# Six raw weight buffers in place of seven, four rounded ones in place of three, and both splits made three units ahead instead of two

## The chip, the cores and the metric

The kernel runs on one core of one Trainium2 chip. The metric is the device time of one execution in microseconds (us). Kernels are compared by runs that alternate on the same chip.

## What is computed

Two layers (`DEPTH = 2`) over 256 context tokens and 256 latent tokens of width 1024. Every matrix product with a large weight is an fp32 product. Cut to what matters:

```
for l in range(DEPTH):
    mod_l, mod_c = split(silu(c) @ w_ada[l] + b_ada[l], 6), split(silu(c_ctx) @ w_ada[l] + b_ada[l], 6)
    h_l, h_c = modulate(rms_norm(x, g), ...), modulate(rms_norm(ctx, g), ...)
    p_l, p_c = split_proj(h_l @ w_in[l]), split_proj(h_c @ w_in[l])
    gla, att, lru = gla_branch(...), attention_branch(...), rglru_branch(...)
    y = sum(sigmoid(gate_i) * (branch_i @ w_branch[l, i]) for i in range(3)) @ w_out[l]
    x = x + mod_l[2] * rms_norm(y, g_post_mix)                 # ctx too, in layer 0
    h = modulate(rms_norm(x, g_pre_ffn), ...)
    u = depthwise_conv(h @ ffn_w_up[l]); g, v = split(u, 2)
    x = x + mod_l[5] * rms_norm((silu(g) * v) @ ffn_w_down[l], g_post_ffn)
```

`w_ada` (1024 x 6144 for each layer) gives the modulation. It is a product with two vectors only, but its weights are 50 MB for the two layers.

## The kernel before

**Units and pairs.** All large weights but `w_ada` are cut into units of 512 KB (`UK = 4` tiles of 128 rows by `UC = 256` columns). Two units (six for `down`) make a pair: 256 output columns, summed over all of the input rows, in two banks of PSUM. There are 352 units. Their order is `PAIR_ORDER`, once for each layer: the projections of the branches, then `y`, `g2` and `b2` in turn, `out`, `up` (22 pairs) and `down`. I write `up 2.0` for the first unit of pair `up 2`, and `up 2.1` for its second. Pairs use two places in PSUM in turn (`PAIR[q % 2]`), so a pair can start on TensorE (PE) only when the pair two before it has been taken out of PSUM (`taken`).

**The split.** A product is made of three passes: a weight is split into a rounded part (`whi`, made by ScalarE, ACT, in `hi(u)`, L397) and the rest (`wlo`, made by VectorE, DVE, in `lo(u)`, L743). The raw weight comes by DMA into one of `RAW` buffers, `wlo` is written over it, and `whi` goes to one of `HI` buffers. So a raw buffer is in use from the issue of its DMA until PE has used the unit (`w_unit_used`, `s_used`).

**The ring.** All DMAs of weights are issued by SyncE (SP) in the order of the list `RING`, in which entry n uses raw buffer `n % RAW`. SP waits before each until the entry that had the buffer before is done with:

```
for n, (kind, v, r) in enumerate(RING):
    s = n % RAW
    if n >= RAW:
        prev, pv, pr = RING[n - RAW]
        if prev == "w":
            sp_.wait_ge(s_used, pv + 1)
        else:
            sp_.wait_ge(s_round, 2 * pv + pr // 2 + 1)
```

**The modulation weights in the ring.** While layer 0 runs from `y 0` to `down 0`, 20 chunks of `w_ada` pass through the same buffers, one for every four units. Let B be the unit at which a chunk is based (`ADA_RUN`: `y 0.0`, `y 2.0`, `g2 0.0` to `g2 3.0`, `out 0.0`, `out 2.0`, `up 0.0`, `up 2.0` to `up 20.0`, `down 0.0`). A chunk has four entries a0 to a3 of 512 KB. PE uses a0 and a1 in a round behind unit B (`ada_round`, L1195) and a2 and a3 in a second round behind unit B+1, and it sends the result through a small product (`ada_pick`, L1204) behind unit B+3. In the ring a0 and a1 stand behind the weights of B+2, and a2 and a3 behind those of B+3. PE runs its instructions in order: a round that waits for its DMA holds everything behind it.

**Edges.** ACT and DVE run their parts of the stream at an `edge(u)` for each unit. ACT's is this (DVE's is alike, with `lo` for `hi`, and with `copy_rows` and `take_mod` of the modulation chunk placed by `u + LEAD - 4` and `u + LEAD - 6`):

```
if q >= 0:
    evac_first(q)
if u + LEAD < NU:
    hi(u + LEAD)
if q >= 0:
    evac_second(q)
```

`q` is the pair that ended with unit u-1, if one did. So a pair is taken out of PSUM at the edge of the unit behind it, and the rounded part of unit u + `LEAD` is made at the edge of u. ACT and DVE run in order too. `hi(u)` waits for the raw buffer's DMA, and for `s_used >= u - HI + 1`.

Of the kernel before, what the change touches and what calls it, by code (L numbers as in the profile page):

```python
# [34 lines left out]
D_FF = 2816  # L35
FT = D_FF // P
UK, UC = 4, 256
RAW, HI, LEAD = 7, 3, 2


PCOLS = {}
# [1622 lines left out]
```

## Time and profile before

| | |
|---|---|
| Three runs | 2107.59 us median (2105.42 to 2109.31) |
| The profiled execution | 2108.57 us, its span 2106.7 us |
| PE busy | 1975.7 us, 94% |
| PE weight load busy | 1605.9 us, 76% |
| DVE busy | 1130.2 us, 54% |
| ACT busy | 940.5 us, 45% |
| DMA, mean | 116 GB/s; 352 raw weight DMAs and 80 of `w_ada`, 512 KB each |
| Chain that ended last | PE 81%, DVE 10%, ACT 5%, issue 2%, DMA 1% |

Busy is the time in which an engine runs instructions; matmuls are pipelined and their ends are modelled. The span is that of the slowest core's instructions, and the execution's time is 1.9 us more.

### The profile page before, as it was taken

How to read it: one execution, taken by the hardware profiler on the slowest of the kernel's cores; microseconds unless marked ns; L12 is line 12 of the kernel's file. 1: busy time of each engine (PE TensorE's matmuls, PEld its weight loads, DVE VectorE, ACT ScalarE, POOL GpSimd, SP SyncE). 2: the span in 40 equal slices, each digit the busy share in tenths (PEclk: the TensorE clock that was granted, in tenths of full speed). 3: DMA queues.
4: the chain of work that ended last, by engine and by line, in shares of the span. 5: the costliest groups of instructions: out<-in, count | busy, mean ns of one | idle time of the engine just before them, and what ended most of it. 6: DMA issues, size and time to landing. Idle time of an engine off the chain costs nothing.

```text
span 2106.7 us, 26324 instructions
## 1 busy us (share of the span) xinstructions
PE 1975.7 (94%) x10944; PEld 1605.9 (76%) x10944; DVE 1130.2 (54%) x1617; ACT 940.5 (45%) x1301; POOL 18.3 (1%) x49
## 2 busy tenths in 40 slices
PE   4999999999999999799999998799898999989997
PEld 1878766777777777477777786588676888979997
DVE  2566455544645333455555323666545678657864
ACT  2343344454654322333333223444343787546653
POOL 1000000000000000000000000000000000000000
PEclk8999999999999999999999999899999999999999
DMA  7211111123332544235444433121221444545663
GB/s 285 61 61 51 56 50 41 49 92 95 96 97 85 177 170 163 104 105 177 169 175 175 167 101 94 41 71 60 76 60 51 155 156 154 177 125 161 181 187 103
DMA packets 67510, 244.97 MB, mean 116 GB/s; under 512 B 7600, under 2 KB 8640, under 8 KB 67264
## 3 DMA queue, kind: packets, MB, share of 16 engines
q1 hardware_dynamic: 64544, 233.86, 34.1%
q0 software_dynamic: 1696, 5.24, 0.8%
q10 hardware_dynamic: 1152, 4.19, 0.5%
q8 instruction: 87, 1.43, 0.3%
q14 instruction: 31, 0.25, 0.0%
HBM read 242.21 MB, written 1.05 MB: 115 GB/s over the span
## 4 chain that ended last, share of the span: by engine, by line
PE 81%; DVE 10%; ACT 5%; issue 2%; DMA 1%; SPq 0%; ACTq 0%; DVEq 0%
PE ps L1264 61%; PE ps L1254 4%; PE ps L1195 2%; PE ps L1540 2%; PE ps L1450 2%; DVE wlo L743 1%; PE ps L1284 1%; DMA wraw<-in_weights 1%; DVE state L1004 1%; PE ps L1471 1%; PE ps L1204 1%; PE ps L1364 1%; ACT whi L397 1%; PE ps L1374 1%; PE ps L1351 1%
## 5 line engine op out<-in xcount | busy, mean ns | idle before, releaser
L743 DVE TENSOR_TENSOR wlo<-wraw,whi 128x1024 fp32r<-128x1024 f32 x352 | 429.6, 1223 | 497.2 <-ACT whi L397 496.7
L397 ACT ACTIVATE whi<-wraw 128x1024 fp32r<-128x1024 f32 x352 | 370.9, 1055 | 396.4 <-PE ps L1264 252.0
L1264 PE MATMUL ps<-hh,whi 128*128 128x512 f32 (+1 forms) x1760 | 416.5, 359 | 25.2 <-DVE hl L860 23.2
L1264 PE MATMUL ps<-hl,whi 128*128 128x512 f32 (+1 forms) x1760 | 399.0, 349 | 0.0
L1264 PEld LDWEIGHTS ps<-hh,whi 128*128 128x128 f32 x1760 | 293.3, 194 | 101.8 <-issue 64.2
L1264 PE MATMUL ps<-hh,wlo 128*128 128x512 f32 (+1 forms) x1760 | 365.5, 349 | 1.8 <-DVE wlo L743 1.8
L1264 PEld LDWEIGHTS ps<-hl,whi 128*128 128x128 f32 x1760 | 295.9, 192 | 42.5 <-issue 2.2
L1264 PEld LDWEIGHTS ps<-hh,wlo 128*128 128x128 f32 x1760 | 286.1, 191 | 44.5 <-issue 4.4
L771 DVE SCALAR_TENSOR_TENSOR fa<-ps,par,fa 128x510 f32<-128x510 f32 (+1 forms) x176 | 100.0, 610 | 14.5 <-ACT fa L460 12.9
L1264 PE MATMUL ps<-bh,whi 128*128 128x512 f32 (+1 forms) x384 | 85.2, 344 | 0.4 <-ACT whi L397 0.4
L460 ACT ACTIVATE fa<-ps,par 128x512 f32<-128x512 f32 (+1 forms) x88 | 54.0, 664 | 69.1 <-PE ps L1264 69.0
L1264 PE MATMUL ps<-bl,whi 128*128 128x512 f32 (+1 forms) x384 | 82.2, 336 | 0.0
L1264 PE MATMUL ps<-fh,whi 128*128 128x512 f32 (+1 forms) x352 | 78.9, 342 | 0.0
L1264 PE MATMUL ps<-fl,whi 128*128 128x512 f32 (+1 forms) x352 | 76.7, 336 | 0.0
L1264 PE MATMUL ps<-bh,wlo 128*128 128x512 f32 (+1 forms) x384 | 74.4, 336 | 0.0
L1264 PEld LDWEIGHTS ps<-bh,whi 128*128 128x128 f32 x384 | 62.4, 190 | 13.8 <-issue 6.2
L749 DVE COPY ada_rows<-ps 128x512 f32<-128x512 f32 x24 | 16.6, 690 | 104.3 <-PE ps L1195 104.3
L1264 PE MATMUL ps<-fh,wlo 128*128 128x512 f32 (+1 forms) x352 | 68.8, 336 | 0.0
L1264 PEld LDWEIGHTS ps<-bl,whi 128*128 128x128 f32 x384 | 62.5, 190 | 7.6
L1264 PEld LDWEIGHTS ps<-bh,wlo 128*128 128x128 f32 x384 | 60.8, 190 | 7.5
L1264 PEld LDWEIGHTS ps<-fh,whi 128*128 128x128 f32 x352 | 57.5, 190 | 9.7 <-issue 3.1
L1264 PEld LDWEIGHTS ps<-fl,whi 128*128 128x128 f32 x352 | 57.6, 190 | 6.9
(206 smaller groups left out, 2392.8 us busy)
## 6 DMA issues: line engine op xcount, KB each, us to landing
wraw<-in_weights SPq DMA_DIRECT2D x352, 512.0 KB, 3.6
wada<-in_w_ada SPq DMA_DIRECT2D x80, 512.0 KB, 4.3
ada_first<-in_w_ada ACTq DMA_DIRECT2D x8, 512.0 KB, 18.5
ada_first<-in_w_ada SPq DMA_DIRECT2D x8, 512.0 KB, 19.9
wgate<-in_w_gate POOLq DMA_DIRECT2D x16, 256.0 KB, 2.8
x<-in_xt SPq DMA_DIRECT2D x1, 2048.0 KB, 9.9
out_x<-x SPq DMA_DIRECT2D x1, 1024.0 KB, 4.5
par<-in_params POOLq DMA_DIRECT2D x1, 370.0 KB, 9.4
```

The costliest lines, as they stand in the source:

```text
L397: A_(whi[u % HI][:], wraw[RING_W[u] % RAW][:], ACT.Copy).then_inc(s_hi, 1)
L460: ins = A_(fa[j][:, f, c0:], pair_[:, f, c0:], ACT.Identity, scale=pcol(l, "fw")[:, t + 2 * FT:t + 2 * FT + 1], bias=pcol(l, "fb")[:, t:t ...
L743: V.tensor_tensor(wlo[s][:], wraw[s][:], whi[u % HI][:].bitcast(F32), ALU.subtract).then_inc(s_lo, 1)
L771: return V.scalar_tensor_tensor(o[:, :, a], v[:, :, b], pcol(l, name)[:, tile:tile + 1], o[:, :, a], ALU.mult, ALU.add)
L1004: ins = V.scalar_tensor_tensor(state[:, d, p + 1], state[:, d, p], g_end[:, d, c:c + 1], kv_, ALU.mult, ALU.add)
L1195: ins = mm(ps[32 * j:32 * j + 32, k if k < 4 else 5, :], csil32[:, 4 * r + j, :], w[:, j % 2, :], start=r == 0, stop=r == 1, tile_position ...
L1204: ins = mm(ps[:, 4, 2 * f:2 * f + 2], ada_rows[:, f * P:(f + 1) * P], pick[:], start=True, stop=True)
L1254: ins = mm(dst[:, r // 2, 256 * (r % 2):256 * (r % 2 + 1)], x_[:, UK * h + kk, r * P:(r + 1) * P], w[:, kk, :], start=first, stop=h == m - ...
L1264: ins = mm(dst[:, r, c:], w[:, kk, r * P:(r + 1) * P], x_[:, UK * h + kk, c:], start=h == 0 and k in (0, 2) and kk == 0, stop=h == m - 1 a ...
L1284: ins = mm(ps[:, 6, c0:], ones[:], src[:, k, c0:], start=k == 0, stop=k == KT - 1)
L1450: ins = mm(ps[:, 4 + t, 0:(g + 1) * CTX], aq[:, h, r0:r0 + P], ak[:, h // (AQ // AKV), 0:(g + 1) * CTX], start=True, stop=True)
L1540: ins = mm(ps[:, 4 + 2 * d + g], wgate[:, 2 * d + g, :], xc[:, n, :], start=True, stop=True)
```

## The change

One line:

```diff
-RAW, HI, LEAD = 7, 3, 2
+RAW, HI, LEAD = 6, 4, 3
```

A buffer has 4 KB in each partition on both sides, so all that lies behind the buffers in SBUF stays where it was. `hi(u + LEAD)` waits at edge u for `s_used >= u` before and after the change. No instruction is added or removed. What is waited for moves, and so does the place of both splits in their engines' rows.

The waits of the ring follow from the code above. For the entries around a base B (before: the entry seven back, now: six back):

| entry | waits for, 7 buffers | waits for, 6 buffers |
|---|---|---|
| w(B+2) | a0 of the chunk before | a1 of the chunk before |
| a0 | a1 of the chunk before | w(B-1) |
| a1 | w(B-1) | a2 of the chunk before |
| w(B+3) | a2 of the chunk before | a3 of the chunk before |
| a2 | a3 of the chunk before | w(B) |
| a3 | w(B) | w(B+1) |
| w(B+4) | w(B+1) | w(B+2) |
| w(B+5) | w(B+2) | a0 |
| w(B+6) | a0 | a1 |

Each row of SP below is one DMA. `wraw` is a unit's weight and `wada` an entry of a chunk. `w_unit_used` is a wait for a unit, `ada_rounds_done` one for a round. The place is base B = `up 2.0`. The rows are w(B+2), a0, a1, w(B+3), a2, a3, w(B+4), w(B+5), w(B+6). Before:

```order
L325 DMA wraw3_57<-in_weights 128x1024 [waits ada_rounds_done]
L327 DMA wada4_72<-in_w_ada 128x1024 [waits ada_rounds_done]
L327 DMA wada5_73<-in_w_ada 128x1024 [waits w_unit_used]
L325 DMA wraw6_60<-in_weights 128x1024 [waits ada_rounds_done]
L327 DMA wada0_68<-in_w_ada 128x1024 [waits ada_rounds_done]
L327 DMA wada1_69<-in_w_ada 128x1024 [waits w_unit_used]
L325 DMA wraw2_56<-in_weights 128x1024 [waits w_unit_used]
L325 DMA wraw3_57<-in_weights 128x1024 [waits w_unit_used]
L325 DMA wraw4_58<-in_weights 128x1024 [waits ada_rounds_done]
```

The same nine DMAs of SP now:

```order
L325 DMA wraw0_54<-in_weights 128x1024 [waits ada_rounds_done]
L327 DMA wada1_67<-in_w_ada 128x1024 [waits w_unit_used]
L327 DMA wada2_68<-in_w_ada 128x1024 [waits ada_rounds_done]
L325 DMA wraw3_57<-in_weights 128x1024 [waits ada_rounds_done]
L327 DMA wada4_70<-in_w_ada 128x1024 [waits w_unit_used]
L327 DMA wada5_71<-in_w_ada 128x1024 [waits w_unit_used]
L325 DMA wraw0_54<-in_weights 128x1024 [waits w_unit_used]
L325 DMA wraw1_55<-in_weights 128x1024 [waits ada_rounds_done]
L325 DMA wraw2_56<-in_weights 128x1024 [waits ada_rounds_done]
```

The order stands; a2 now waits for a unit, and w(B+5) for a round.

On ACT at the same place, before: `hi` of B+3, the first part of the evacuation of `up 2` (`fa0`, at the edge of B+2), `hi` of B+4, the rest of the evacuation, `hi` of B+5, and the evacuation of `up 3`.

```order
L397 ACTIVATE whi1_76<-wraw6_60 128x1024 [waits w_unit_used,raw_full6]
L460 ACTIVATE fa0_129<-ps,par 128x512 [waits split_pairs_made,w_unit_used]
L460 ACTIVATE fa0_129<-ps,par 128x512
L397 ACTIVATE whi2_77<-wraw2_56 128x1024 [waits w_unit_used,raw_full2]
L480 ACTIVATE fs0_131<-fa0_129 128x512 [waits pair0_taken]
L482 ACTIVATE fh_127<-fa0_129 128x512 [waits product_made]
L397 ACTIVATE whi0_75<-wraw3_57 128x1024 [waits w_unit_used,raw_full3]
L460 ACTIVATE fa1_130<-ps,par 128x512 [waits split_pairs_made,w_unit_used]
```

And now:

```order
L397 ACTIVATE whi0_72<-wraw0_54 128x1024 [waits w_unit_used,raw_full0]
L460 ACTIVATE fa0_127<-ps,par 128x512 [waits split_pairs_made,w_unit_used]
L460 ACTIVATE fa0_127<-ps,par 128x512
L397 ACTIVATE whi1_73<-wraw1_55 128x1024 [waits w_unit_used,raw_full1]
L480 ACTIVATE fs0_129<-fa0_127 128x512 [waits pair0_taken]
L482 ACTIVATE fh_125<-fa0_127 128x512 [waits product_made]
L397 ACTIVATE whi2_74<-wraw2_56 128x1024 [waits w_unit_used,raw_full2]
L460 ACTIVATE fa1_128<-ps,par 128x512 [waits split_pairs_made,w_unit_used]
```

The `hi` ahead of the evacuation of `up 2` was that of B+3 and is now that of B+4, whose weight is the DMA into `wraw0` above.

On DVE at the start of layer 0, ahead of the first use of the modulation, before:

```order
L911 TENSOR_TENSOR lrl<-lrw,lrh 128x8x2x16
L743 TENSOR_TENSOR wlo_61<-wraw_54,whi_75 128x1024
L743 TENSOR_TENSOR wlo_62<-wraw_55,whi_76 128x1024
L749 COPY ada_rows<-ps 128x512
L755 TENSOR_TENSOR mod<-ps,par 128x8
```

And now:

```order
L911 TENSOR_TENSOR lrl<-lrw,lrh 128x8x2x16
L743 TENSOR_TENSOR wlo_60<-wraw_54,whi_72 128x1024
L743 TENSOR_TENSOR wlo_61<-wraw_55,whi_73 128x1024
L743 TENSOR_TENSOR wlo_62<-wraw_56,whi_74 128x1024
L749 COPY ada_rows<-ps 128x512
```

A third split stands ahead of `copy_rows(0)` (L749).

## Rows read from the trace of the kernel before

**Rows 1.** The page: TensorE busy, and its granted clock in 40 slices.
```profile
PE 1975.7 (94%) x10944; PEld 1605.9 (76%) x10944; DVE 1130.2 (54%) x1617; ACT 940.5 (45%) x1301; POOL 18.3 (1%) x49
PEclk8999999999999999999999999899999999999999
```

**Rows 2.** Waits of PE, whole span: us in total, times, longest.
```profile
PE ps L1264 <- DVE hl L860: 23.2, 3, 9.7
...
PE ps L1264 <- DVE wlo L743: 1.8, 1, 1.8
...
PE ps L1264 <- ACT whi L397: 0.9, 2, 0.5
```

**Rows 3.** Waits of ACT, stretch 645 to 1205 us.
```profile
ACT whi L397 <- DMA wraw<-in_weights: 139.5, 43, 8.7
```

**Rows 4.** Timeline around base `up 2.0`: start, length, what [idle before, releaser].
```profile
939.19 1.07 PE L1195 MATMUL ps<-wada,csil 128*32 128x512 f32 x8
939.29 7.47 SPq L325 DMA_DIRECT2D wraw<-in_weights  x3
...
940.19 1.20 PE L1264 MATMUL ps<-hh,whi 128*128 128x512 f32 x4
...
942.95 1.06 ACT L397 ACTIVATE whi<-wraw 128x1024 fp32r<-128x1024 f32 x1 [2.20 <-DMA wraw<-in_weights]
...
945.77 1.07 PE L1264 MATMUL ps<-hh,whi 128*128 128x512 f32 x4
...
949.57 1.06 ACT L397 ACTIVATE whi<-wraw 128x1024 fp32r<-128x1024 f32 x1 [3.03 <-DMA wraw<-in_weights]
...
951.41 1.45 ACT L460 ACTIVATE fa<-ps,par 128x512 f32<-128x512 f32 x2 [0.78 <-PE ps L1264]
...
952.01 1.19 PE L1264 MATMUL ps<-hh,whi 128*128 128x512 f32 x4
...
952.89 2.85 DVE L771 SCALAR_TENSOR_TENSOR fa<-ps,par,fa 128x510 f32<-128x510 f32 x4 [1.00 <-ACT fa L460]
```

**Rows 5.** The tile `wada`: time from the issue of a DMA to its landing.
```profile
DMA to landing us min/median/max: 3.3/4.3/7.0
```

**Rows 6.** DMA issues at 738.24 to 739.09 us, three together: the last.
```profile
wada<-in_w_ada SPq DMA_DIRECT2D x1, 512.0 KB, 5.9
```

**Rows 7.** Timeline in `out 3`, base `out 2.0`: PE's sum of squares, and ACT.
```profile
863.73 1.88 PE L1284 MATMUL ps<-sqm,ones 128*128 128x512 f32 x4
...
865.57 1.06 ACT L397 ACTIVATE whi<-wraw 128x1024 fp32r<-128x1024 f32 x1 [5.55 <-DMA wraw<-in_weights]
```

**Rows 8.** Timeline behind `b2 3` (813.74 on), and behind `out 3` (869.28 on).
```profile
813.74 0.33 SPq L327 DMA_DIRECT2D wada<-in_w_ada  x1
...
821.03 1.20 PE L1264 MATMUL ps<-mh,whi 128*128 128x512 f32 x4
...
869.28 1.02 ACT L449 ACTIVATE sqm<-ps 128x1024 f32<-128x1024 f32 x1 [2.65 <-PE ps L1264]
...
871.10 1.06 ACT L397 ACTIVATE whi<-wraw 128x1024 fp32r<-128x1024 f32 x1
```

**Rows 9.** Timeline of the start.
```profile
33.23 2.48 DVE L743 TENSOR_TENSOR wlo<-wraw,whi 128x1024 fp32r<-128x1024 f32 x2 [5.39 <-ACT whi L397]
...
36.35 1.87 PE L1204 MATMUL ps<-pick,ada_rows 128*128 128x2 f32 x8 [7.10 <-DVE ada_rows L749]
```

**Rows 10.** Timeline: two idle stretches of PE.
```profile
283.72 1.12 PE L1437 MATMUL ps<-asq,ones 128*128 128x512 f32 x2 [1.26 <-ACT asq L617]
...
1523.12 3.46 PE L1450 MATMUL ps<-ak,aq 128*128 128x512 f32 x4 [3.09 <-ACT prob L633]
```

**Rows 11.** Stretches behind them: length, busy of the five engines, PEclk (granted clock), DMA, GB/s.
```profile
1522.90:1526.30 3.40, 3.18 (x4) 1.39 (x5) 1.05 (x3) 0.08 (x1) 0.00 (x0) 0.52 0.00 0
...
283.00:287.00 4.00, 3.28 (x13) 2.42 (x14) 3.24 (x6) 2.27 (x5) 0.00 (x0) 1.00 0.00 0
```

## The prediction

> **What bounds the kernel now.** I read the page first. PE is busy for 1975.7 us of a span of 2106.7, and its granted clock is at 0.8 or more of full speed in every slice [rows 1]. So PE is the bound, and the change can only gain what PE idles for the splits, or lose by making it idle. The waits of PE come next: it waits 1.8 us once for `wlo` and 0.9 us for `whi` in the whole span [rows 2]. The largest wait of its products is for `hl`, 23.2 us, at the norms, and no buffer of weights helps that. A split that is made one unit earlier is worth at most 2.7 us.
>
> Then I ask where the ring of raw buffers is short. In the stretch of the 20 modulation chunks (645 to 1205 us) ACT waits 43 times, 139.5 us in all, for a raw DMA in front of `hi` [rows 3]. PE feels none of it. The timeline around base B = `up 2.0` shows why. SP issues w(B+4) at 939.29, when B+1 has ended, and its `hi` starts at 942.95, 3.66 us later. The next one is issued when B+2 ends (PE starts B+3 at 945.77) and its `hi` starts at 949.57, 3.8 us later. PE starts B+4 at 952.01 [rows 4]. So ACT waits for DMAs that were issued one or two units ahead, and the slack that is left before PE is about one unit, 5.6 us. Outside of the chunks the ring has no such entries, and a weight has units to land in.
>
> **The change, part by part.**
>
> *The split one unit earlier.* `hi(u + LEAD)` waits for the same unit of PE as before. It gives PE at most the 2.7 us above. I take 0, since that wait is spread over three places, and I keep 2.7 as the bound of a gain.
>
> *a3 is issued behind unit B+1 instead of behind B.* PE needs a3 in the second round, right behind B+1. Before, it had a whole unit to land in. Now SP issues it when the last matmul of B+1 is done, the moment at which PE turns to the round. That is 939.29 in these rows. It lands 3.6 us later if it goes as w(B+4) did (942.95 less 939.29, less the start of `hi`), so at 942.9. The round and its gap take 1.0 us now (939.19 to 940.19), and half of it needs a3. PE would go on to B+2 at 942.9 + 0.5 = 943.4, not at 940.19: 3.2 us. All 20 chunks do this, as the ring's table is the same for each: **20 x 3.2 = 64 us**. The bounds are the least and the median landing of a `wada`, 3.3 and 4.3 us [rows 5]: 2.9 and 3.9 us, or 58 and 78. The median is of DMAs that were issued in twos and threes, and a3 goes alone, so I stay near the low end.
>
> The Trainium skill has a price for a DMA (DMA: Bandwidth & Descriptors, section Anatomy of one DMA): 2.0 us and the bytes by 436 GB/s, measured on the GpSimd path. For 512 KB that is an estimate of 3.2 us, where the trace has 3.6; by it this term would be 56 us. Its rule to issue a DMA early and to wait late speaks against the change, which does the opposite twice.
>
> *w(B+4) is issued behind B+2 instead of B+1, and its `hi` now stands ahead of the evacuation of pair B.* ACT reaches `hi` of B+4 at the edge of B+1 and stays there until the DMA lands. The evacuation (edge of B+2) is queued behind it, and so is DVE's, whose `lo(B+4)` waits for that `hi`. PE needs the pair out of PSUM before it starts B+4. For `up`: `hi` can start where the row has 949.57, since the DMA behind B+2 is issued at the same moment as there. It takes 1.06, ACT's two `fa` 1.45, DVE's four `fa` 2.85 [rows 4]: 949.57 + 1.06 + 1.45 + 2.85 + 0.1 for the handovers is 955.0. PE would start at 952.01. That is 3.0 us, 11 times (`up 0` to `up 20`, every second): **33 us**. For the two bases in `out`, PE needs ACT's squares of pair B even earlier, for the sum of squares within B+3. `hi` would start at 865.57, the time of the row, end at 866.63, the squares take 1.02, which is 867.7 against 863.73 [rows 7, 8]: 4.0 us each, **8 us**. For `g2` and `y` the evacuation is one ACT instruction of the size of that square, so it is done at about 949.57 + 1.06 + 1.1 = 951.7, ahead of 952.01: 0, or up to 1 us where a load of ACT's function table comes with it. I take **1 us** for all six. `down 0` has six units and no pair to take out there: 0.
>
> *w(B+7) comes behind two `wada`.* With `LEAD` 3, ACT makes `hi(B+7)` at the edge of B+4. Its DMA is now the third of three that SP issues together when B+3 ends. Three together now land late: issued at 738.24, 738.61 and 739.09, the last needs 5.9 us [rows 6], so it is there 6.8 us after the first was issued. PE needs the unit far later, but what is queued behind it on ACT matters twice. Behind `b2 3` stands the last split of `mixed` (`mh` and `ml`, of the size of `hi`, 1.06, and `lo`, 1.24): 813.74 + 6.8 + 1.06 + 1.06 + 1.24 = 823.9, and PE needs it for `out 0.1` at 821.03 [rows 8]: 2.9 us. Behind `out 3` stands the norm, on which PE waits: `hi` would start at 869.28 + 6.8 = 876.1, not at 871.10 [rows 8]: 5.0 us. Together **8 us**.
>
> *Start.* DVE's third `lo` stands ahead of `copy_rows(0)`, and PE waits 7.10 us for just that copy [rows 9]. Two `lo` take 2.48 [rows 9], so a third is **1 us** more (1.2).
>
> *The clock.* The terms so far make PE idle for about 3 us, 20 + 11 + 2 + 1 = 34 times. What short idles do to the clock is in the trace: after an idle of 3.09 us the granted clock is 0.52 over 3.4 us, which is PE's level of 1.2 GHz in place of 2.4, and after one of 1.26 it stays at 1.00 [rows 10, 11]. The stalls are as long as the first of these, and 3.4 us at half speed cost 1.7 us of work. Part of the slow stretch can lie within the idle (in the row it begins at 1522.9, and PE starts at 1523.12), so I take 1.3 us a stall: 34 x 1.3 = **44 us**. The bounds are 0 (as after the idle of 1.26) and 34 x 1.7 = 58.
>
> *Layer 1 and the rest of layer 0.* No chunks there. A weight is issued when the unit six back is done, and its `hi` is due at the end of the unit four back: two units. Layer 1's units are about half as long (256 columns in place of 512), so two are about 5.8 us against a landing of 3.6. What hides the lost buffer is that slack. If DMAs bunch up, ACT waits a little and PE still has three units: 0, with 5 us as the bound.
>
> **Sum.** 64 + 33 + 8 + 1 + 8 + 1 + 44 = 159 us on the profiled execution's 2108.6 (1.0 above the median of the runs): 2267.6, so **2267 us**, 7.5% slower.
>
> **The rivals.**
> - *The ring's stalls without the clock's part* (0.2). For it: the stalls lie between long stretches of dense matmuls (four units and more from one to the next), and the row of 3.09 us is from the attention stage, with more small waits around it. Then 2108.6 + 115 = 2224 us.
> - *Worse than the main case* (0.1): a3 and w(B+4) land as slowly as the `wada` median, and the slow clock stretches are whole: +14 + 9 + 14, which is 2305 us.
> - *Only a3 stalls; the evacuation finds its way* (0.05). For it: ACT's wait is hidden for `g2` and `y` already, so I may have counted it too long for `up`. 64 + 20 x 1.3 and 10 for the rest: 2208 us.
> - *No change, since all DMAs are hidden anyway* (0.03). For it: PE waits for no DMA now, and ACT takes 139.5 us of such waits without harm. Against it: that harmlessness is the unit of slack which both edits take away. 2108 us.
> - *Faster, because the split is what PE waits for* (0.01). If the stalls of 2.7 us hide more that the waits put down to others, such as ACT and DVE that run late in the attention stage, an earlier split could give 10 us: 2098. It decides only if a3 lands before PE turns to the second round, against the table of the ring.
>
> **How the numbers follow.** The main case has 0.61; the rivals hold the rest. The likeliest case gives the time, 2267. The range must hold 8 in 10: from 2219 (stalls without the clock, with a3 at its least) up to 2295 (full slow stretches, and half of the slower landings). A measurement of this kernel tells 0.2%, about 4 us, from no change. Faster 0.01, same 0.03, slower 0.96.
>
> **What would show it.** Right: PE waits for `wada` DMAs 20 times, 3 us each, at L1195; the start of each second `up` pair is released by DVE's `fa`; ACT's waits for raw DMAs grow to more than 250 us; the granted clock falls below 1.00 between 670 and 1300 us; layer 1 is as long as before. Wrong: a second round that starts its second half within 1 us, which would mean that a3 was issued earlier than the ring's table says; or a granted clock of 1.00 throughout, which takes away 44 us; or stalls in layer 1, which I hold to be free.

## The result, and the profile after

The change makes the kernel slower: 2287.07 us (2282.62 to 2289.79, 4 runs) against 2107.39 us of the kernel before on the same chip (2105.42 to 2109.31, 4 runs). The ratio is 1.0844, with a 95% interval from 1.0829 to 1.0860. The forecast was 2267 us, with a range from 2219 to 2295. The profiled execution took 2282.62 us, its span is 2280.6, and its mean granted clock is 0.953 (0.976 before).

The page of the changed kernel: busy time, the granted clock in 40 slices, and the chain that ended last.

```profile
PE 2044.3 (90%) x10944; PEld 1635.2 (72%) x10944; DVE 1130.7 (50%) x1617; ACT 934.3 (41%) x1301; POOL 18.2 (1%) x49
...
PEclk8999999999999999798998999989999999998999
...
PE 73%; DVE 11%; DMA 7%; ACT 6%; issue 3%; SPq 0%; ACTq 0%; DVEq 0%
```

The same 10944 matmuls keep PE busy for 68.6 us longer than in [rows 1]. No work was added. Some 21 us of it are second rounds that now run in two halves, one after the other: 1.05 us for each half (rows further below), where all eight matmuls took 1.07 together [rows 4]. The other 48 us are matmuls at a lower clock. The rest of the difference is idle time of PE. It stands in the waits of PE (us in total, times, longest):

```profile
PE ps L1195 <- DMA wada<-in_w_ada: 54.0, 20, 2.8
PE ps L1264 <- DVE fa L771: 30.4, 11, 2.8
PE ps L1264 <- DVE hl L860: 24.3, 4, 9.7
...
PE ps L1284 <- ACT sqm L449: 8.7, 4, 3.9
...
PE ps L1264 <- DVE ml L823: 4.2, 2, 3.7
```

Only the third of these has its counterpart of like size in the kernel before [rows 2]. The first two are new: 20 waits for a DMA of the second round, 11 for the evacuation. The timeline around base B = `up 2.0` shows one of each (compare [rows 4]):

```profile
1013.88 1.05 PE L1195 MATMUL ps<-wada,csil 128*32 128x512 f32 x4
1013.98 0.33 SPq L327 DMA_DIRECT2D wada<-in_w_ada  x1
...
1017.68 1.92 PE L1195 MATMUL ps<-wada,csil 128*32 128x512 f32 x4 [2.75 <-DMA wada<-in_w_ada]
1019.53 1.75 PE L1264 MATMUL ps<-hh,whi 128*128 128x512 f32 x4
...
1025.86 1.28 SPq L325 DMA_DIRECT2D wraw<-in_weights  x3
...
1029.38 1.06 ACT L397 ACTIVATE whi<-wraw 128x1024 fp32r<-128x1024 f32 x1 [19.51 <-DMA wraw<-in_weights]
1030.35 1.43 ACT L460 ACTIVATE fa<-ps,par 128x512 f32<-128x512 f32 x2
...
1031.81 2.84 DVE L771 SCALAR_TENSOR_TENSOR fa<-ps,par,fa 128x510 f32<-128x510 f32 x4
...
1034.71 2.08 PE L1264 MATMUL ps<-hh,whi 128*128 128x512 f32 x4 [2.65 <-DVE fa L771]
```

The reader should see two chains of events. SP issues a3 at 1013.98, while PE is already in the round that needs it, and it lands 3.7 us later. Then w(B+4) is issued at 1025.86, when the last matmul of B+2 has ended. ACT waits at its `hi` until 1029.38, and the evacuation of the pair, for which B+4 waits, comes behind it. Before, the `fa` of ACT did not wait for that `hi`.

The stretches behind both idles (length, busy of the five engines, granted clock, DMA, GB/s):

```profile
1017.60:1021.00 3.40, 3.32 (x8) 1.43 (x9) 0.69 (x1) 0.00 (x0) 0.00 (x0) 0.53 0.00 0
1034.70:1038.10 3.40, 3.39 (x9) 2.71 (x10) 2.45 (x4) 2.30 (x4) 0.00 (x0) 0.54 0.67 272
672.20:1379.90 707.70, 589.68 (x2410) 416.93 (x2410) 246.59 (x328) 174.60 (x218) 0.56 (x1) 0.91 0.35 117
```

The first two are the slow clock of [rows 11] (0.52, the level of 1.2 GHz), now behind idles of 2.75 and 2.65 us. It does not come behind each idle. In all 11 waits for `fa` and in 15 of the 20 for a3 the granted clock of the 3.4 us behind lies between 0.50 and 0.74. In the other five, with idles just as long (2.61 to 2.75 us), it stays at 1.00. One of these, with the stretch behind it:

```profile
875.02 1.05 PE L1195 MATMUL ps<-wada,csil 128*32 128x512 f32 x4 [2.75 <-DMA wada<-in_w_ada]
...
874.97:878.37 3.40, 3.35 (x14) 2.10 (x15) 0.69 (x1) 0.00 (x0) 0.00 (x0) 1.00 0.00 0
```

So what the clock costs is an average over idles that cost it and idles that do not. The third stretch above is the whole stage of the chunks. The same stage of the kernel before:

```profile
669.00:1203.80 534.80, 518.04 (x2410) 386.03 (x2410) 248.34 (x328) 182.19 (x219) 0.56 (x1) 0.98 0.45 155
```

It grew by 172.9 us, from 534.8 to 707.7. So nearly all of the loss is in this stage: 71.6 us more busy time (the split rounds and the lower clock), and 101.3 us more idle time of PE. It starts 3.2 us later than before, and what follows it takes 900.7 us in place of 902.9.

### The profile page after: what moved, and what is told of

It reads as the page before. It is cut to its first block, busy times and chain, and to the rows that moved or that the text cites. A ratio compares the mean times of both kernels' runs of the same rounds, so it can differ in the third digit from the quotient of the medians.

```text
span 2280.6 us, 26322 instructions
## 1 busy us (share of the span) xinstructions
PE 2044.3 (90%) x10944; PEld 1635.2 (72%) x10944; DVE 1130.7 (50%) x1617; ACT 934.3 (41%) x1301; POOL 18.2 (1%) x49
## 3 DMA queue, kind: packets, MB, share of 16 engines
q8 instruction: 87, 1.43, 0.3%
HBM read 242.21 MB, written 1.05 MB: 107 GB/s over the span
## 4 chain that ended last, share of the span: by engine, by line
PE 73%; DVE 11%; DMA 7%; ACT 6%; issue 3%; SPq 0%; ACTq 0%; DVEq 0%
PE ps L1264 54%; DMA wraw<-in_weights 4%; PE ps L1254 4%; DMA wada<-in_w_ada 3%; PE ps L1195 2%; PE ps L1540 2%; DVE wlo L743 1%; PE ps L1450 1%; DVE fa L771 1%; PE ps L1284 1%; DVE state L1004 1%; PE ps L1471 1%; PE ps L1364 1%; ACT whi L397 1%; PE ps L1374 1%
## 5 line engine op out<-in xcount | busy, mean ns | idle before, releaser
L397 ACT ACTIVATE whi<-wraw 128x1024 fp32r<-128x1024 f32 x352 | 370.1, 1054 | 671.1 <-DMA wraw<-in_weights 455.4
L1264 PE MATMUL ps<-hh,whi 128*128 128x512 f32 (+1 forms) x1760 | 429.0, 368 | 54.4 <-DVE fa L771 27.7
L1264 PE MATMUL ps<-hl,whi 128*128 128x512 f32 (+1 forms) x1760 | 409.0, 356 | 0.0
L1264 PEld LDWEIGHTS ps<-hh,whi 128*128 128x128 f32 x1760 | 302.2, 199 | 140.8 <-issue 71.2
L1264 PEld LDWEIGHTS ps<-hl,whi 128*128 128x128 f32 x1760 | 303.3, 196 | 45.5 <-issue 2.2
L1195 PE MATMUL ps<-wada,csil 128*32 128x512 f32 x320 | 74.4, 665 | 54.0 <-DMA wada<-in_w_ada 54.0
L749 DVE COPY ada_rows<-ps 128x512 f32<-128x512 f32 x24 | 16.6, 691 | 178.7 <-PE ps L1195 178.7
L1264 PE MATMUL ps<-fh,whi 128*128 128x512 f32 (+1 forms) x352 | 80.6, 348 | 2.7 <-DVE fa L771 2.7
L1195 PEld LDWEIGHTS ps<-wada,csil 128*32 128x32 f32 x320 | 9.7, 110 | 87.5 <-DMA wada<-in_w_ada 73.4
```

Source lines behind the costliest of these rows:

```text
L397: A_(whi[u % HI][:], wraw[RING_W[u] % RAW][:], ACT.Copy).then_inc(s_hi, 1)
L1195: ins = mm(ps[32 * j:32 * j + 32, k if k < 4 else 5, :], csil32[:, 4 * r + j, :], w[:, j % 2, :], start=r == 0, stop=r == 1, tile_position ...
L1264: ins = mm(dst[:, r, c:], w[:, kk, r * P:(r + 1) * P], x_[:, UK * h + kk, c:], start=h == 0 and k in (0, 2) and kk == 0, stop=h == m - 1 a ...
```

## The experiments

Theory A is that of the prediction: three mechanisms add up, a3 that is issued too late, splits that stand ahead of the evacuation, and the slow clock behind the idles. Its rivals were that the clock costs nothing here, that one raw buffer fewer is the cause in itself, and that the place of the splits costs little.

Each ratio is to the kernel before on the run's own chip: 2109.68 us for runs 1 to 4, 2108.70 for 5 to 8, and 2111.00 for 9 and 10. Differences in us between runs of different groups, or between a run and the changed kernel (2107.39 beside it), are of times that were not taken side by side. Reckoned by the ratios they come out up to 3.5 us otherwise.

**1. The lead of three undone (`e1_lead2`).** The diff is against the changed kernel, as in all that follow.

```diff
-RAW, HI, LEAD = 6, 4, 3
+RAW, HI, LEAD = 6, 4, 2
```

> Six raw buffers and four rounded ones as in the changed kernel, but both splits two units ahead again. Theory A (the ring makes a3 late; the evacuation of pair B is late because a split that waits for w(B+4) stands ahead of it): the late a3 stays, 20 times 3.8 us and 1.4 us of slow clock behind each, and the 11 waits of PE for DVE's fa are gone, those in out and behind b2 3 too: 2107 + 76 + 28 = about 2211 us. Theory B (the third unit of lead itself is what costs, and the ring is harmless): about 2107 us. Theory C (the ring alone, in which the order on ACT and DVE plays no part): 2287 us, as the changed kernel.

Measured: 2209.27 us (2203.0 to 2211.62), ratio to the kernel before 1.0459 [1.0438, 1.0480]. Waits of PE:

```profile
PE ps L1195 <- DMA wada<-in_w_ada: 52.8, 20, 2.8
```

The waits for a3 stand, those for `fa` are gone. So the third unit of lead costs 77.8 us of the changed kernel (2287.07 less 2209.27; 81 by the ratios), and the rest comes with six raw buffers. ACT waits for raw DMAs 325.6 us here (144.4 in the kernel before, whole span), and only what stands in front of PE counts.

**2. Six buffers without the late a3 (`e2_lead2_ring`).** The two `wada` pairs are entered in the ring one weight earlier.

```diff
-RAW, HI, LEAD = 6, 4, 3
+RAW, HI, LEAD = 6, 4, 2
-    for _b, _r in ((_u - 2, 0), (_u - 3, 2)):
+    for _b, _r in ((_u - 1, 0), (_u - 2, 2)):
```

> As the run before (6 raw, 4 rounded, two units ahead), and the four entries of a modulation chunk stand one unit earlier in the ring, so that a3 waits for unit B again and not for B+1, while w(B+3) waits for B+1. Theory A: a3 has a unit to land in, w(B+3) lands 3.6 us after B+1's end and its split is done before PE needs it: no stall and no slow clock in the chunks, 2105 to 2115 us with one raw buffer less. Rival (six buffers are too few for the traffic of this stage, whatever the order): still over 2180 us.

Measured: 2104.18 us (2101.84 to 2105.06), ratio 0.9972 [0.9960, 0.9984]. PE waits for no `wada`; the longest sum among its waits is the one of before:

```profile
PE ps L1264 <- DVE hl L860: 23.2, 3, 9.7
```

One raw buffer fewer costs nothing in this order. What costs is which entry it makes late. The changed line of the ring is worth 105.1 us (2209.27 less 2104.18), or 5.25 us for each of 20 chunks.

**3. PE kept busy while it waits for a3 (`e3_fill`).** The waits stay as in the changed kernel. 13 matmuls on data at hand, into a bank of PSUM that nothing reads, stand between the halves of each second round. All the work of the kernel is still done.

```diff
+                    if k >= 4 and r == 1 and j == 2:
+                        fill(FILL)
```

with, at the head of the file and in PE's program,

```diff
+FILL = 13
...
+            def fill(n):
+
+                for _ in range(n):
+                    mm(ps[:, 7, :], hh[:, 0, 0:P], hh[:, 0, :], start=True, stop=True)
```

> The changed kernel with 13 matmuls of 512 columns (2.9 us at full clock) added to TensorE in each of the 20 second rounds, between the half that has its data and the half that waits for a3. Their results go to an unused bank of PSUM. If the slow clock behind the stalls is what makes them cost more than their length, TensorE stays at full clock there and the kernel gets faster by 20 times 1.4 us although it has 260 matmuls more: about 2259 us. If the rest of the cost is something else behind a wait (a restart, or more waiting), 2287 us or slower.

Measured: 2258.60 us (2258.0 to 2263.24), ratio 1.0707 [1.0691, 1.0723], mean granted clock 0.964. The timeline of one round:

```profile
1004.97 1.05 PE L1203 MATMUL ps<-wada,csil 128*32 128x512 f32 x4
1005.96 3.25 PE L1192 MATMUL ps<-hh 128*128 128x512 f32 x13
1009.13 1.05 PE L1203 MATMUL ps<-wada,csil 128*32 128x512 f32 x4
1010.12 1.20 PE L1272 MATMUL ps<-hh,whi 128*128 128x512 f32 x4
```

With 260 matmuls more the kernel is 28.5 us faster than the changed one. The four matmuls behind the wait take 1.05 us and the first four of the unit 1.20, where they took 1.92 and 1.75. So the rival without a clock's part falls, and the clock costs at least 28.5 / 20 = 1.4 us an a3 stall, on average. It is "at least", since the 13 matmuls last longer than the wait: the second half starts 4.16 us after the round (1009.13 less 1004.97), and 3.80 in the changed kernel.

**4. Also busy while it waits for the evacuation (`e4_fill_both`).** As 3, and 11 more such matmuls ahead of B+4 at the 11 bases of `up` that stall.

```diff
+                    if name in ("up", "down") and h == 0 and u - 4 in ADA_RUN and (name, i) != ("up", 0):
+                        fill(11)
```

> As the run before, and 11 more such matmuls (2.5 us) ahead of the first unit of every second up pair and of down 0, where TensorE waits for DVE's fa, 11 times. By the clock theory 31 stalls keep their length and lose the slow stretch: 2287 - 31 x 1.45 = about 2242 us, with a granted clock of about 0.97 in place of 0.95. Without it, 2287 us or slower.

Measured: 2247.57 us (2244.09 to 2247.84), ratio 1.0646 [1.0630, 1.0662], clock 0.973. Another 11.0 us come back, 1.0 for each of the 11. The expected time, 2242, is missed by 5.6 us, and the traces account for a part of that only. The fills take 2.80 us and delay B+4 by 0.1 us at `up 2.0`, some 1.3 us if it is so at all 11. And in run 3, where these waits stand without a fill, two of the 11 left the clock at 1.00, so that a fill had nothing to give back there. Both fills together give back 39.5 us net.

**5. The split behind the evacuation (`e5_order`).** The lead of three stays for all units but w(B+4), whose split on ACT and DVE goes one edge back, where a lead of two has it.

```diff
-                if u + LEAD < NU:
+                if u - 2 in ADA_RUN:
+                    hi(u + LEAD - 1)
+                if u + LEAD < NU and u - 1 not in ADA_RUN:
                     hi(u + LEAD)
```

and the same for `lo` on DVE.

> The changed kernel (6, 4, 3) with its ring, but at the two edges behind a chunk's base the split of B+4 stands behind the evacuation of pair B on ACT and DVE, and not ahead of it. Theory A: the 11 waits of TensorE for DVE's fa (2.8 us), those for the squares in out (two, 3.9 us) and the slow clock behind them go, the 20 late a3 stay: 2287 - 31 - 8 - 1 - 13 x 1.4 = about 2229 us. Rival (the late landing of w(B+4) itself is what holds the evacuation or unit B+4): 2287 us.

Measured: 2229.47 us (2217.02 to 2230.66), ratio 1.0558 [1.0529, 1.0587]. Waits of PE:

```profile
PE ps L1199 <- DMA wada<-in_w_ada: 54.0, 20, 2.9
```

No wait for `fa` is left, those for the squares in `out` are as short as before (1.2 us in all at that line, 8.7 in the changed kernel), and 57.6 us come back. The head of ACT's row is what stops the evacuation, as theory A has it. What stays between this and run 1 (20.2 us) belongs to the other effects of the lead. The two traces differ by 18.3 us. 13.1 of these are in the stage of the chunks, where w(B+7) at `b2 3` (3.73 us) and at the norm (11.17 us for 6.87) still makes PE wait. 2.0 us are ahead of the stage and 3.1 behind it.

**6 and 7. Where the 5.5 us come from by which run 2 is below the kernel before on its chip (`e6_hi3_ring`, `e7_raw7_ring`).** Both have the moved ring. The first has three rounded buffers, the second also seven raw ones, which leaves only the changed line of the ring.

```diff
-RAW, HI, LEAD = 6, 4, 3
+RAW, HI, LEAD = 6, 3, 2
```

```diff
-RAW, HI, LEAD = 6, 4, 3
+RAW, HI, LEAD = 7, 3, 2
```

> 6 raw and 3 rounded buffers, two units ahead, with the chunk's entries one unit earlier in the ring. If the fourth rounded buffer is what made 6, 4, 2 with that ring faster than the kernel before, this one is back at 2107 to 2110 us; if the ring's order or the lost raw buffer did it, 2104 us as that run.

> The kernel before (7, 3, 2) with only the chunk's entries one unit earlier in the ring. TensorE waited for no weight in the chunks before, so the order alone should give nothing: 2107 to 2110 us. 2104 us would put the small gain on the order of the ring.

Measured: 2109.52 us (2107.93 to 2112.59, 11 runs), ratio 1.0005 [0.9996, 1.0014], and 2108.62 us (2107.34 to 2113.12, 11 runs), ratio 1.0005 [0.9996, 1.0014]. With seven raw buffers the order of the ring is worth nothing, and in the moved order the seventh raw buffer is worth nothing. The fourth rounded buffer is: 5.3 us, or 0.3%, by run 2 against run 6. It shortens a wait of ACT, here of run 6:

```profile
ACT whi L397 <- PE ps L1264: 230.9, 94, 6.1
```

and of run 2, with four:

```profile
ACT whi L397 <- PE ps L1264: 80.6, 33, 6.1
```

The code says why. `hi(u + LEAD)` waits for `s_used >= u + LEAD - HI + 1`. That is u-1 with four buffers and a lead of two, but u with three and two and also with four and three. In the changed kernel the longer lead uses up what the fourth rounded buffer gives, and this wait of ACT stands at 215.7 us, 90 times. Layer 1, which has no chunks, shows the same. Measured from the end of the wait for `hl` of 9.67 or 9.68 us, with which it begins, to the end of the span, it takes 770.0 us in both run 6 and the kernel before, and 768.5 in run 7 (all three and two). It takes 765.7 to 765.8 in runs 1, 2 and 8 (four and two), and 767.9 to 772.1 in the changed kernel and runs 3, 4, 5, 9 and 10 (four and three). The rows from which it is measured, of runs 6 and 2, whose spans are 2106.2 and 2102.2:

```profile
1336.23 1.20 PE L1264 MATMUL ps<-hh,whi 128*128 128x256 f32 x4 [9.67 <-DVE hl L860]
```

```profile
1336.53 1.19 PE L1264 MATMUL ps<-hh,whi 128*128 128x256 f32 x4 [9.68 <-DVE hl L860]
```

By which of PE's waits the shorter wait of ACT reaches PE is not shown.

**8. A better version (`e8_start`).** As run 2, and at the start DVE makes its first splits behind the second of the copies for which PE waits.

```diff
-                    for u in range(LEAD):
-                        lo(u)
                     for half in range(2):
                         for k in (2 * half, 2 * half + 1):
                             copy_rows(k)
+                            if k == 1:
+                                for u in range(LEAD):
+                                    lo(u)
```

> 6, 4, 2 with the ring moved, and at the start DVE's two lo stand behind the second copy_rows and not ahead of the first. TensorE waited 7 to 8 us there for that copy, which by the trace of the kernel before could start at 29.3 us (when the first two rounds end) and starts at 35.6. If that copy is the bound at the start, up to 6 us less than 2104: 2098 to 2101 us. If TensorE's next round waits for its own weights (landing at 38 us) whatever DVE does, 2104 us.

Measured: 2097.30 us (2095.39 to 2100.39, 5 runs), ratio 0.9949 [0.9937, 0.9962]. The first use of the modulation comes at 28.93 us, where [rows 9] has 36.35:

```profile
28.93 1.05 PE L1205 MATMUL ps<-pick,ada_rows 128*128 128x2 f32 x8
```

This beats both kernels, the one before by 0.5%. It is 6.9 us below run 2, or 4.8 by the ratios, since the two ran on different chips. In the traces the first unit starts at 48.07 us for 56.04. The gain comes from the place in DVE's row that the prediction priced for a third `lo`.

**9 and 10. How much idle the clock bears, and what a wait hides (`e9_fill4`, `e10_fill22`).** As run 3 with 4 and with 22 matmuls in place of 13.

> The changed kernel with 4 added matmuls in each second round in place of 13, so that TensorE still idles some 1.9 us of the 2.8. By the rows of the kernel before, an idle of 1.95 us was enough to bring the clock down, and one of 1.26 was not. If that holds here, most of the slow stretches stay: 2275 to 2287 us. If it takes the full 2.8 us of idle, 2259 us, as with 13.

> The changed kernel with 22 added matmuls (4.9 us) in each second round, which is longer than the wait for a3 (about 3.3 us from the end of the first half). TensorE then is what is waited for: 13 matmuls are free, the 7 or so beyond the wait cost 0.22 us each, 20 times: about 2259 + 20 x 1.6 = 2291 us. If a3 landed later than the profile shows, it would be less.

Measured with 4: 2261.70 us (2259.90 to 2264.71), ratio 1.0717 [1.0700, 1.0733]. The idle that is left:

```profile
1007.68 1.20 PE L1192 MATMUL ps<-hh 128*128 128x512 f32 x4
1010.51 1.05 PE L1203 MATMUL ps<-wada,csil 128*32 128x512 f32 x4 [1.64 <-DMA wada<-in_w_ada]
1011.49 1.20 PE L1272 MATMUL ps<-hh,whi 128*128 128x512 f32 x4
```

The expectation was that much of the slow clock would stay, since an idle of 1.95 us in the kernel before had brought it. It did not: behind 19 of the 20 idles, of 1.43 to 1.67 us, the matmuls go at full speed (1.05 and 1.20 here), and 25.4 of the 28.5 us come back. The twentieth, of 1.68 us, has the slow clock behind it:

```profile
1177.64 1.79 PE L1203 MATMUL ps<-wada,csil 128*32 128x512 f32 x4 [1.68 <-DMA wada<-in_w_ada]
1179.37 2.04 PE L1272 MATMUL ps<-hh,whi 128*128 128x512 f32 x4
```

So shorter idles bring the slow clock less often, and neither this run nor the changed kernel gives a length at which it begins. Measured with 22: 2307.78 us (2304.74 to 2313.01), ratio 1.0929 [1.0908, 1.0950], where 2291 was expected. Nine more matmuls in 20 rounds are 180, and at the 0.25 us of one in the row of run 3 (3.25 / 13) that is 45 us; 49.2 were measured (46.8 by the ratios). So nothing of them is hidden. The wait hides no more than the idle that the trace shows, 2.75 us, and 13 matmuls already fill it. I had reckoned with 3.3 us of cover.

## Why the prediction was right

The changed time was forecast 20 us too low, and each mechanism was there. Three of its signs came too: 20 waits for `wada` at L1195 (2.7 us each, where it said 3), `fa` as what releases each second `up` pair, and 455.4 us of ACT's waits for raw DMAs, where it said more than 250. By its steps:

- **a3 behind B+1**: right, but mis-sized, 76 us for 64. At full clock (a chunk in `g2`) the round shows the size:

```profile
742.34 1.05 PE L1195 MATMUL ps<-wada,csil 128*32 128x512 f32 x4
746.11 1.05 PE L1195 MATMUL ps<-wada,csil 128*32 128x512 f32 x4 [2.71 <-DMA wada<-in_w_ada]
747.09 1.59 PE L1264 MATMUL ps<-bh,whi 128*128 128x512 f32 x4
```

  From the round to the next unit it is 4.75 us in place of the 1.0 of [rows 4], so 3.75 lost (I reckon with 3.8) and not 3.2. Two things were too small. The half that waits starts 3.77 us after the round does (the DMA lands in 3.7, not in 3.6, and is issued 0.1 late), and it takes 1.0 us by itself, not 0.5: a half of four matmuls takes as long as the whole round of eight did in the row of before. That is no matter of PE having idled, since in run 3 the second half follows the fills at once and takes 1.05 us too. The eight ran side by side (in the code the four products of a round go to four strips of 32 rows), and halves that wait for different DMAs do not. So half a round never cost 0.5 us. The Trainium skill (DMA: Bandwidth & Descriptors, Anatomy of one DMA) prices DMAs of the GpSimd path, and the prediction's estimate from it was 3.2 us for 512 KB. This trace has 3.7 for a lone one that SP issued, and the measurement decides:

```profile
wada<-in_w_ada SPq DMA_DIRECT2D x1, 512.0 KB, 3.7
```

- **w(B+4) ahead of the evacuation**: right. In `up`, B+4 starts 8.9 us after B+2 ends, where [rows 4] has some 6.1: 2.8 us, 11 times, 31 us for 33. In `out` the sum of squares waits 3.83 and 3.90 us, 8 us for 8. The first unit behind `y 0` waits 1.0 us for 1.
- **w(B+7) third of three**: right. `b2 3` stalls for `ml` by 3.74 us, with its gap 3.9 (2.9 forecast), and at the norm ACT's `hi` waits 4.28 us, with its gap 4.4 (5.0 forecast):

```profile
864.22 2.04 PE L1264 MATMUL ps<-mh,whi 128*128 128x512 f32 x4 [3.74 <-DVE ml L823]
...
939.05 1.06 ACT L397 ACTIVATE whi<-wraw 128x1024 fp32r<-128x1024 f32 x1 [4.28 <-DMA wraw<-in_weights]
```

- **Not foreseen**: in four chunks of `g2` the first round too waits for its second half, 1.7 us in all, since a1 lands late behind two others.
- **Start**: 2.1 us at the first unit for 1.2, and 3.2 at the start of the stage. PE waits 8.66 us for `copy_rows(0)` (7.10 in [rows 9]).
- **The clock**: 44 us were forecast. The stage grew by 172.9 us, of which the waits above are 76 + 31 + 8 + 1 + 3.9 + 4.4 + 1.7 = 126. The other 47 us are the clock, by subtraction. The busy time gives nearly the same: of its 71.6 us, 20.6 are the split rounds and 1.7 the first rounds, which leaves 49. The experiments bear it out: in runs 1 and 2 an a3 costs 5.25 us, of which 3.8 are its wait, so 1.45 us is the clock (1.3 forecast). Filling the idles gave back 39.5 us net. That 1.3 fits is in part luck. The prediction took every idle to bring the slow clock and some of the slow stretch to lie within the idle. In run 1 three of the 20 idles did not bring it, so the others cost 1.7 us each, the prediction's upper bound.
- **Layer 1 and the raw buffer**: free, as forecast. The time behind the stage is even 2.2 us shorter in this one trace.
- **The split earlier**: taken as 0, and the lead itself has shown no gain. With four rounded buffers layer 1 is 2 to 6 us longer with a lead of three than with two (runs above). The fourth rounded buffer, on which the prediction had no term, is worth something with a lead of two: layer 1 is 4.3 us shorter in run 2 than in run 6.

The sum of what was measured: 126 + 47 in the stage, 3.2 ahead of it and -2.2 behind it is 174.0, the growth of the profiled execution (2282.6 less 2108.6). It must be, as the 47 is what was left over. The forecast had 159; 12 of the 15 us between them are the term of a3. Of the rivals, the one without the clock's part (2224) is out by run 3. "Worse" had the right sign for a3, for the reason that was in none of its terms.

Left open: whether a lead of three is worth anything with seven raw buffers or with five rounded ones. Neither was tried. In layer 1, where no chunk makes an entry late, it was worth nothing with six and four.

## What to carry to other kernels

Before a buffer is taken from a ring, write down for each entry which event frees its slot now, and compare that event with the first use of the entry. A mean slack says nothing: here 352 weights lost nothing, and one entry in each of 20 chunks cost 105 us, which one line of order gave back with six buffers. Work that is pulled ahead in an in-order engine brings its wait with it, so ask what stands behind it in the row. One more buffer and one more unit of lead cancel in what the writer waits for, as they did here. And price an idle of TensorE with its clock: here one of some 2.7 us cost 1.4 us more on average, though some cost nothing.

## What the runs showed that I had not expected

- Idles of PE of 1.43 to 1.68 us left the clock at full speed 19 times of 20 (run 9). Those of 2.56 to 2.85 us in the changed kernel brought the slow clock 26 times of 31 (0.50 to 0.74 over 3.4 us), and the other five, as long, left it at 1.00.
- Matmuls whose results nobody reads make the kernel faster: 260 of them by 28.5 us (run 3), and 80 of them by 25.4 us (run 9).
- Four matmuls of a round by themselves take 1.05 us, as much as the eight of a round without a wait between (1.07 in [rows 4]), be there an idle ahead of them (the changed kernel) or matmuls (run 3). So splitting a round costs 1 us beside the wait.
- A fourth rounded buffer and a lead of three give ACT no more room than three and two: its wait for PE is 215.7 us for 252.0 before, and 80.6 with four and two (run 2).
